# A hybrid decoder layer with expert retrieval: the first chunk's S5 branch by tiles, its root mean square applied after the projection, and four heads ranked alone

## The reference

```
h_t  = abar * h_{t-1} + B u_t            (S5: 32 groups of 64 complex states)
z    = gelu(C h + D u);  a = z * sigmoid(z @ w_glu + b)
b    = rglru(conv4(x_lru)) * gelu(y_lru)
x    = x + (sigmoid(g_a) * (a @ w_proj_a) + sigmoid(g_b) * (b @ w_proj_b)) @ w_out
q    = rmsnorm(x) @ w_q                  (8 heads, 2 halves of 128)
s    = q . sub_keys (128 keys a half); top 16 of each half, top 16 of the 256 sums -> 16 experts
x    = x + sum_k softmax_k * gelu(u_tab[e_k] . x) * v_tab[e_k]
y    = rmsnorm(x)
```

## Time and profile before

| | |
|---|---|
| median of 3 runs | 3243.57 us (3235.98 to 3243.91) |
| the profiled execution: its own time | 3249.83 us |
| its span | 3247.7 us |
| instructions | 31396 |
| busy, TensorE / VectorE / ScalarE / GpSimd | 84% / 77% / 30% / 38% of the span |
| HBM read | 1245.05 MB, mean 385 GB/s over the span |

### The profile page before, as it was taken

How to read it: one execution, slowest core, us unless ns; L and a number is a source line. 1 busy time by engine, 2 the same in 40 slices (tenths; PEclk the granted TensorE clock), 3 DMA queues, 4 the chain that set the end, 5 groups by cost and what they waited for, 6 DMA issues and landing times.

```text
span 3247.7 us, 31396 instructions
## 1 busy us (share of the span) xinstructions
PE 2714.0 (84%) x9120; PEld 1542.8 (48%) x9120; DVE 2493.6 (77%) x5858; ACT 976.4 (30%) x3001; POOL 1225.6 (38%) x1048
## 2 busy tenths in 40 slices
PE   7988988998979989888778989899888895666566
PEld 6874544565445445555334545556434442222122
DVE  6836888888679888887679888887668886666754
ACT  2113433232134332322134332322123432222223
POOL 0003344344343444344343443343344343545553
PEclk9999999999989999999989999998999997878789
DMA  4369999999999999999999999999999999999997
GB/s 136 95 212 396 403 419 420 409 396 419 418 417 385 411 420 419 381 420 419 418 418 400 418 417 403 387 416 374 417 401 418 420 395 298 421 407 421 422 422 332
DMA packets 208636, 1251.68 MB, mean 385 GB/s; under 512 B 27961, under 2 KB 36537, under 8 KB 76369
## 3 DMA queue, kind: packets, MB, share of 16 engines
q0 software_dynamic: 148608, 1082.20, 81.3%
q1 hardware_dynamic: 57344, 158.97, 13.2%
q10 hardware_dynamic: 2512, 8.52, 0.7%
HBM read 1245.05 MB, written 4.55 MB: 385 GB/s over the span
## 4 chain that ended last, share of the span: by engine, by line
DMA 41%; PE 26%; DVE 21%; issue 3%; ACT 3%; DVEq 2%; POOL 2%; ACTq 1%; POOLq 0%
DMA arena<-in_uv,arena 40%; PE psum L1740 13%; DVE arena L1410 10%; PE psum L1661 6%; DVE arena L1015 4%; DVE arena L1007 3%; ACT arena L692 2%; POOL arena L651 2%; PE psum L1784 2%; PE psum L1796 1%; DVE arena L1256 1%; PE psum L1775 1%; PE psum L1674 1%; PE psum L1694 1%; PE psum L1646 1%
## 5 line engine op out<-in xcount | busy, mean ns | idle before, releaser
L1740 PE MATMUL psum<-arena 128*128 128x512 f32 x3192 | 1606.7, 647 | 463.8 <-ACT arena L692 430.8
L651 POOL DMA_INDIRECT arena<-in_uv,arena x1032 | 1221.6, 1184 | 1994.7 <-PE psum L1740 1381.0
L1410 DVE CUSTOM_DVE_ANT_0 arena<-arena 128x1024 f32<-128x1024 f32 x1024 | 1237.2, 1224 | 529.6 <-DMA arena<-in_uv,arena 498.4
L1740 PEld LDWEIGHTS psum<-arena 128*128 128x128 f32 x3192 | 620.2, 202 | 1303.6 <-ACT arena L692 642.1
L692 ACT ACTIVATE arena<-arena 128x128 f32<-128x128 f32 (+3 forms) x2481 | 699.0, 313 | 1633.7 <-DVE arena L1410 1478.4
L1661 PE MATMUL psum<-arena 128*128 128x256 f32 (+1 forms) x2688 | 622.5, 387 | 12.0 <-DVE arena L1015 6.4
L1661 PEld LDWEIGHTS psum<-arena 128*128 128x128 f32 x2688 | 515.4, 193 | 143.5 <-issue 71.3
L1015 DVE SCALAR_TENSOR_TENSOR arena<-arena 128x1024 f32<-128x1024 f32 (+6 forms) x477 | 392.7, 830 | 66.8 <-ACT arena L692 35.9
L1007 DVE TENSOR_TENSOR arena<-arena 128x256 f32<-128x256 f32 (+10 forms) x832 | 285.0, 382 | 24.1 <-issue 1.7
L692 ACT ACTIVATE arena<-psum 128x256 f32<-128x256 f32 (+7 forms) x266 | 107.3, 414 | 554.5 <-PE psum L1661 481.4
L692 ACT ACT_TABLE_LOAD x113 | 145.0, 1283 | 3.9 <-PEq L2040 0.8
(11 more groups left out here) (97 smaller groups left out, 949.4 us busy)
## 6 DMA issues: line engine op xcount, KB each, us to landing
arena<-in_w_in SPq DMA_DIRECT2D x112, 512.0 KB
arena<-in_w_q SPq DMA_DIRECT2D x68, 512.0 KB
arena<-in_w_ab SPq DMA_DIRECT2D x40, 512.0 KB
arena<-in_w_out SPq DMA_DIRECT2D x40, 512.0 KB
arena<-in_uv,arena POOLq DMA_INDIRECT x1032
arena<-in_w_glu SPq DMA_DIRECT2D x16, 256.0 KB
arena<-in_x_tok SPq DMA_DIRECT2D x8, 512.0 KB
arena<-in_keys SPq DMA_DIRECT2D x32, 128.0 KB
```

The costliest lines, as they stand in the source:

```text
L651: pool.indirect_dma_start(uvring[:, r], None, i_["uv"], bass.IndirectOffsetOnAxis(column, 0)).then_inc(uv_in[r], 16)
L1410: V.tensor_tensor_reduce(out=u, in0=u, in1=hn[i // (SLOT // 2)], scale=1.0, scalar=0.0, op0=ALU.mult, op1=ALU.add, accum_out=dots_[:, b % ...
L1740: ins = mm(PV[:, half], dg[:, PAIR * (b % 2) + k], uvring[:, i % UV, at:at + 512], start=(i % (SLOT // 2) == 0), stop=(pe_slots(c, i + 1) ...
```

## The change

It touches the first chunk alone; from the second chunk on, only counts that the first chunk's lists, units and evictions enter are rewritten.

- **Norm.** x arrives in 4 pieces (`x0_in`), ahead of the large parameters; only 5 small loads (`step_in`) and `nmix` are issued before it. VectorE multiplies x by the norm weight alone (`hx_ok`), TensorE projects the 4 `u` blocks from that, and the reciprocal root is applied to `u` at its eviction (`scaled_u`, now on VectorE instead of ScalarE). The other inputs read `hT`, scaled as before but with a second pass of 8 products.
- **S5 by tiles.** `s5_half`, `s5_in_half`, `s5_out_half`, `lru_half` each do one tile: the same number of matmuls and scans a call, with half the columns (64 instead of 128 in the matmuls), and twice as many calls. The first tile's S5 runs beside the 16 gate projections, the second's between the first tile's `mix` and `out`. The RG-LRU gates come after the eighth gate projection; glu, and `a` (now in `rT`), are by tiles.
- **Ranking.** Four heads (`ALONE` = 4) are ranked for tile 0 alone, the other four for both, heads 0 to 3 of tile 1 in two rounds of two heads: 10 rounds instead of 9. `mix` and `out` of tile 1 move behind the first list, beside batches. `w_glu` is loaded twice in the first chunk and 8 query blocks instead of 4 are loaded twice: 92 ring loads instead of 84.
- **Batches.** `OWN0` goes from 48 to 57, so the second chunk's first 96 points have 71 batches beside them, not 80; `on_dve` follows.

```diff
-OWN0 = 48
+OWN0 = 57
+ALONE = 4
+IN_AT, OUT_AT, GATES_AT = (0, 1, 3, 5, 6, 8, 9, 10), (5, 5, 6, 7, 9, 10, 11, 12), 8
...
+X1 = OLD + 15
+def at1_mix(m):
+    return OLD + max(m, 1)
+def at0_q(r):
+    return OLD + 6 * (r - 1) if r < ALONE else OLD + 21 + 6 * (r - ALONE)
...
-    first, whole, last = (32, 82, 108) if c else (48, 90, 111)
+    first, whole, last = (32, 82, 108) if c else (57, 94, 112)
...
-            weights0 = trunk + mix + out + mix[0:4] + query[0:2] + mix[4:6] + query[2:4] + mix[6:8] + out \
-                + query[4:16] + query[0:4]
+            weights0 = trunk + mix + out + query[0:2 * ALONE] + trunk[28:32] + mix + out \
+                + query[2 * ALONE:] + query[0:2 * ALONE]
...
+                    if l == 48:
+                        sp.wait_ge(lru_ok, blocks(1))
+                        sp.dma_start(x_tok[:, 0], i_["x_tok"][P:2 * P, :]).then_inc(tok_in, 16)
...
+            def scaled_u(q):
+                dve.wait_ge(unit, U_U + q + 1)
+                tt(halves(uS[:, q, 0:C]), parities(PB[q % 2][:, 0:C]), parities(rstd[:, 0:C]), ALU.mult).then_inc(ue_ok, 1)
...
+                pieces(gates[0], 2 * QT)
+                pieces(gates[1], QT)
+                pieces(scans[1], 1)
+                a_half(E_GLU0, EARLY)
+                pieces(scans[1], 2)
                 for m in range(KT):
-                    mix(m, U_MIX0 + m, early, MIXB[m % 2])
+                    mix(m, U_MIX0 + m, EARLY, MIX0B[m % 2])
+                    pieces(scans[1], 1)
+                pieces(scans[1], 13)
+                pieces(gates[1], QT)
                 dve.wait_ge(unit, U_OUT0 + KT)
...
+            def s5_in_half(k, jp):
+                q, done = jp // 2, SJ // 2 * k + jp
+                need(pe, bu_read, done)
+                pe.wait_ge(ue_ok, q + 1)
+                for j in (2 * jp, 2 * jp + 1):
+                    o = 32 * (j % 4)
+                    for part in range(2):
+                        for r in range(2):
+                            at, src = 2 * SEG * part + SEG * k, 2 * SEG * r + SEG * k
+                            ins = mm(SB[j % 2][:, at:at + SEG], wT[o:o + 32, QT * (2 * r + part) + q],
+                                     uS[o:o + 32, q, src:src + SEG], start=(r == 0), stop=(r == 1))
+                ins.then_inc(bu_ok, 1)
...
                 for k in range(KT):
-                    out(0, U_OUT0 - 8 + k, k, [(0, P, 0)])
-                for m in range(3):
-                    mix1(m)
+                    if k % 2:
+                        s5_in_half(1, 4 + k // 2)
+                        s5_out_half(1, 3 + k // 2)
+                    out(0, 40 + k, k, [(0, P, 0)])
+                s5_out_half(1, 7)
                 pe.wait_ge(hn_ok, 1)
...
                     if h == 2:
                         soft(0, P, 1, alone)
```

More of the change, by code:

```diff
@@ L100, in at_gate, with at_ga @@
     return AT_GATE + q
-def at_ga(m, first):
-    return 2 + 3 * m if first else 22 + 27 * m // 16
+def at_ga(m):
+    return 22 + 27 * m // 16
 def at_mix(m):
@@ L179, in lists, with pairs, blocks, second_at @@
 def lists(c):
-    return HEADS * c + 1 if c else 0
+    return ROUNDS0 + HEADS * (c - 1) if c else 0
+def pairs(c):
+    return SJ // 2 * (c + 1) if c else 0
+def blocks(c):
+    return QT * (c + 1) if c else 0
+def second_at(c):
+    return SECOND_AT if c else X1 - OLD + 5
 def mixes(c):
@@ L376, in build @@
         hn = [R.take(D) for _ in range(2)]
-        acc = [R.take(D) for _ in range(2)]
+        acc = [R.take(D)]
+        acc1_at = R.at
+        acc.append(R.take(D))
         dg = R.take(2 * PAIR, P)
@@ L477, in build @@
         MIXB = [SB, YB]
+        MIX0B = [[psum[:, 6 + k, P * side:P * side + P] for side in range(2)] for k in range(2)]
+        EARLY, LATE, BOTH = slice(0, P), slice(P, C), slice(0, C)
         PV = psum[:, 6:8, :]
@@ L812, in columns_of, with glu @@
                     act.sem_inc(tr_ev, 1)
+                def glu(k, u, cols):
+                    act.wait_ge(lru_ok, QT * (k + 1))
+                    for q in range(QT):
+                        projected(u + q, rT[:, q, cols], PB[q % 2][:, 0:P], ACT.Tanh, scale=0.5, bias=bglu[:, q:q + 1])
+                act.wait_ge(set_a, 1)
+                af(e1, e0, ACT.Tanh)
+                af(ztmp[:, :, 1], ztmp[:, :, 0], ACT.Exp)
+                act.drain()
+                act.sem_inc(set_b, 1)
@@ L814, in first_lists @@
+                glu(0, U_GLU0, EARLY)
+                for q in range(QT):
+                    z_half(1, q)
                 square_sum(0, 0, P, PVf)
@@ L1090, in _ @@
                 lambda: tt(e4, th, e3, ALU.subtract),
+            )
+            dve.wait_ge(rt_ok, 1)
+            V.reciprocal(rstd[:, 0:C], rstd[:, 0:C])
+            dve.drain()
+            scaled_u(0)
+            scaled_u(1)
+            for k in range(KT):
+                tt(hT[:, k, 0:C], gb[:, k, 0:C], rstd[:, 0:C], ALU.mult).then_inc(hT_ok, 1)
+            scaled_u(2)
+            chain(
                 lambda: tt(q0, bt3(e3), taub, ALU.mult),
@@ L1551, in chunk @@
                     sample_states()
-                if first:
-                    for q in range(QT):
-                        conv(c, q, last)
-                    V.tensor_copy(xl[:, :, 0:3], xl[:, :, C:C + 3]).then_inc(halo_ok, 1)
-                    c_tables()
                 scans = (piece for jp in range(SJ // 2) for piece in s5(c, jp))
@@ L1565, in chunk @@
                         next(gates)
-                    elif not first:
+                    else:
                         conv(c, convs, last)
@@ L1624, in chunk @@
                     dve.sem_inc(i8_ok, 1)
-            for c in range(CH):
+            first_chunk()
+            for c in range(1, CH):
                 chunk(c, c == CH - 1)
```

697 lines of the change are left out of this document (441 added, 256 removed).

## The result

| | before | after |
|---|---|---|
| median | 3243.03 us (4 runs, 3235.98 to 3243.91) | 3273.3 us (4 runs, 3271.61 to 3274.12) |
| ratio after / before | | 1.0096, 95% interval 1.0080 to 1.0112 |
| profiled execution: time, span | 3249.83, 3247.7 | 3272.53, 3270.7 |

The changed kernel is slower by 30 us, 20 more than forecast and 7 above the range. A second measurement, among the experiments, gave 1.0074 (1.0060 to 1.0089), +24 us (28 between its medians). So the traces can explain 23 us, and the other 7.6 of the 30 lie between executions of one kernel.

What follows compares the result with a forecast made beforehand. It took the run as a dependent chain up to the first gather at 251.1 us, then full DMA. Gather 9 us earlier, added bytes +7.8, moved bytes +11.3: +10 us, median 3243.6 to 3253.7, range 3234 to 3266.

Steps and rivals of the forecast that it cites:

- Where the first gather goes: Walk through the chain from the start to the first gather: it comes at 242 us, 9 us earlier, range 236 to 247.
- half the columns in half the time: Rival on `s5_in_half`: 0.86 us a call, first gather at 228, total 3241 us, no change; chance 0.12.
- What the DMA pays: Behind the first gather: 2.9 MB of added weights cost 7.8 us, 4.2 MB moved there cost 11.3 us.
- The ring rival: TensorE freeing gather slots, not DMA, sets the pace: added and moved bytes cost nothing, 3230 to 3235 us; chance 0.17.
- -9 + 7.8 + 11.3: Whole run: earlier first gather, added bytes and moved bytes, in us, giving +10 us.
- the share after it 1.01 as before: Behind the first gather: the DMA engines' busy share stays at 1.01, as in the kernel before.
- The later start of the second chunk: Rival: its first 96 points crowd into 71 batches instead of 80, 8 us more, 3262 us; chance 0.14.
- TensorE busy over 97%: Sign that would decide for the crowded second chunk: TensorE's busy share over 97% in that stretch.
- Clock loss: Rival: waits in the gates, between pairs and before queries at half clock; first gather at 250, 3260 us; chance 0.09.
- Of the 30 us gained by 148, the second tile's S5 gives back nearly all: Between the gate loop's end at 148 us and tile 0's residual, put at 215 against 216.7 before.
- the loop of 82 us: TensorE's 16 gate projections with the first tile's S5 and the RG-LRU gates: from 67 to 148 us.
- four pairs of 6.2 us: Output products with a pair of the second tile's S5 between every two: 27 us, from 181 to 208.

Runs made afterwards that it cites:

- copy_late: Kernel before plus 16 unneeded DRAM-to-DRAM copies of 512 KB beside the second chunk's first weight loads: 3265.75 us, 1.0064 against the kernel before.
- own57: Kernel before with the second chunk starting 57 steps after the first gather instead of 48, VectorE's limits following: 3257.43 us, 1.0036 against the kernel before.
- s5_whole: Changed kernel with S5 of both tiles back in the gate loop, by whole chunk: 3253.47 us, 1.0026 against the kernel before.
- whole_fill: Changed kernel with S5 by whole chunk, and values between the second tile's transposes and their eviction: 3247.52 us, 1.0008 against the kernel before.
- hold: Kernel before with one wait, so weights from slot 60 on start only when the first list is ready: 3261.52 us, 1.0055 against the kernel before.

## Why the prediction was wrong

- **Where the first gather goes: right.** 244.2 against 242; every station within some 2 us. Of the rivals, half the columns in half the time is out: 1.60 us for 16 records, where I took 1.7 between bounds of 0.86 and 3.1. The Trainium skill's "TensorE: Matmul & The Clock Gate", section "LDWEIGHTS (loading the stationary operand)", gives a time that follows the weights' columns and not the moving ones, and the trace agrees within 7%: 100 ns a record against its 107.
- **What the DMA pays: right in MB and price.** 2.88 MB added (2.9), 33.83 MB ahead of the first gather (33.8), and `copy_late` gives 2.5 us/MB (1.9 to 3.1) where I used 2.70 and 2.44. The ring rival, at 0.17, falls with that run.
- **The step that failed is the sum**, -9 + 7.8 + 11.3: it had terms for the start and for bytes behind the first gather but none for DMA share lost there, since it took "the share after it 1.01 as before" for granted. It was 0.99 and 0.98 up to gather 256, some 14 to 16 us. Two losses of this kind were in the change. The later start of the second chunk: I had it as a rival at +8 and 0.14, and `own57` with its variants measured 6 to 12. The rival's sign, TensorE busy over 97%, did not come (90% in `own57`); the loss did. It was not another way for the change to go but a term that comes on top of the forecast, whatever the rest does. The second tile's norm beside the gathers: 5 to 6 us, in no case of mine. I had walked TensorE's row up to the first gather and stopped there, though the change moved this place from 280 to 370 us, and the wait for the transposes' eviction (`tr_ev`), with no values ahead of it, stands in the code.
- The sum with these: -6.9 + 7.8 + 11.2 + (6 to 12) + (5 to 6) = 23 to 30, against 24 and 30 measured. The same sum with the first gathers of `s5_whole` and `whole_fill` gives 9 to 16 and 5 to 11, against 8 and 3 measured (intervals 5.5 to 11.7 and -0.6 to 5.5): it holds at its low end, so in the changed kernel crowding costs nearer 6 us than 12. It leaves no room there for moved bytes that cost more than their price, as in `hold`, but the two weren't separated. The split between the terms is thus shown less well than their total.
- **Clock loss** (rival at 0.09) was there, 3.79 and 2.75 us for 16 records from 225 us and 0.50 at 370, but as an amplifier of waits. The forecast had the first of them in its walk, at the right size.
- "Of the 30 us gained by 148, the second tile's S5 gives back nearly all" was right in its outcome and should have been followed up: `s5_whole` shows that the split itself costs 14.7 us at the first gather.
- Two sums of the walk are loose: from 67 us the loop of 82 us ends at 149, not 148, and four pairs of 6.2 us are 25 us, where the walk has 27. The trace has 27.2 there, from 183.0 to 210.2, so the station came out right by a number that its own terms don't give.

## What to carry to other kernels

Where a resource is full only because work runs ahead of it, sum up three things: when it starts, what it must carry, and each place behind the start where a change lets the feeding engine wait with nothing to hand on; read the changed order there too, not only up to the start. Mechanisms that don't exclude each other belong into the sum, not among the rivals. Price both halves of a split matmul before you make it: with weights of 128 columns, going from 128 to 64 moving columns saved 6% here (1.71 to 1.60 us), so work that rides along whole should not be cut in two to start one half earlier.

## What the runs showed of the hardware that I had not expected

- A copy from DRAM to DRAM behind the first gather cost 2.5 us per MB copied (1.9 to 3.1), although each MB is read and written: no more, within that interval, than the 2.44 to 2.70 us for a MB loaded to SBUF.
- Holding back 2.9 MB of weights by some 12 us cost 18 us, 10 of them as DMA share that went missing, and 7 of these 10 only at 300 to 320 us (share 0.63), some 50 us behind the moment at which the held transfers began.
- The profiled execution of the kernel before stood 6.8 us above its median, and runs of before in one group of 12 to 23 spread over 12 to 17 us (at most from 3237.66 to 3254.51), so that effects of 5 us are at the edge of what four to eleven runs can tell apart.
